# Units of the attention between the gate products in pairs, turned four slots behind their scores and met with the values six slots behind

## The reference

```python
h = rms_norm(x, norm_mix_g)
z = h @ w_in
u, v, q, k, va, gate_a, gate_b = jnp.split(z, SPLITS, axis=-1)
ya = spatial_gating_mixer(u, v, ...) @ w_proj_a
yb = window_attention(q, k, va, q_norm_g, k_norm_g, sink) @ w_proj_b
merged = jax.nn.sigmoid(gate_a) * ya + jax.nn.sigmoid(gate_b) * yb
x = x + merged @ w_out
x = x + hierarchical_moe(rms_norm(x, norm_ffn_g), ...)

# window_attention, for one head and one block of 128 queries against 3 blocks of keys
s = jnp.einsum('bqgrd,bkgd->bgrqk', qi, ki) * scale
s = jnp.where(valid, s, NEG)
p = jax.nn.softmax(jnp.concatenate([s, sink_l], axis=-1), axis=-1)[..., :-1]
o = jnp.einsum('bgrqk,bkgd->bqgrd', p, vi)
```

## Time and profile before

| | |
|---|---|
| median of three runs | 2125.69 us (2124.58 to 2127.52) |
| the profiled execution, its own time | 2126.55 us |
| its span, first to last instruction | 2124.7 us |
| PE busy | 2085.5 us, 98% of the span |
| VectorE, ScalarE, GpSimd busy | 1278.3, 1072.9 and 466.3 us (60%, 50%, 22%) |
| chain of work that ended last | PE 48%, DMA 6%, VectorE 2%, ScalarE 2% |
| mean granted clock of TensorE | 0.997 of 2.4 GHz |

### The profile page before, as it was taken

One profiled execution on the slowest core, in us unless ns is written; L12 is line 12 of the kernel. 1 busy time (PEld: TensorE's weight loads), 2 busy tenths in 40 slices (PEclk: granted clock), 3 DMA queues, 4 the chain that ended last, 5 costly groups with the idle time before them and its releaser, 6 DMA issues.

```text
span 2124.7 us, 30272 instructions
## 1 busy us (share of the span) xinstructions
PE 2085.5 (98%) x10268; PEld 1730.8 (81%) x10268; DVE 1278.3 (60%) x1645; ACT 1072.9 (50%) x1584; POOL 466.3 (22%) x653
## 2 busy tenths in 40 slices
PE   8999999999999999999999999999999999999997
PEld 7788888888788888897888888767888788888886
DVE  5654233465554233455653434458998899999995
ACT  5453332343542332344533232137877788888884
POOL 4251011210451011203510102012222222212221
PEclk9999999999999999999999999999999999999999
DMA  8312323443123322452122225489999978996863
GB/s 230 95 41 90 99 80 99 140 168 100 59 52 122 99 80 85 168 174 70 40 90 90 80 83 195 174 302 380 378 371 361 363 283 275 380 386 239 317 237 68
DMA packets 108658, 379.46 MB, mean 179 GB/s; under 512 B 13506, under 2 KB 19827, under 8 KB 82964
## 3 DMA queue, kind: packets, MB, share of 16 engines
q1 hardware_dynamic: 91812, 335.64, 44.1%
q0 software_dynamic: 16752, 42.56, 7.6%
HBM read 402.78 MB, written 34.60 MB: 206 GB/s over the span
## 4 chain that ended last, share of the span: by engine, by line
PE 48%; DMA 6%; DVE 2%; ACT 2%; issue 1%; POOL 0%; POOLq 0%; SPq 0%; ACTq 0%; DVEq 0%
DMA held_wu<-w_up_e 5%; PE main L518 3%; PE main L520 3%; PE main L519 3%; PE main L1975 3%; PE main L1973 3%; PE main L1974 3%; PE aux L1973 3%; PE aux L1974 3%; PE aux L1975 3%; PE main L1987 3%; PE main L1989 2%; PE main L1988 2%; PE main L506 2%; PE main L508 2%; PE main L507 2%
## 5 line engine op out<-in xcount | busy, mean ns | idle before, releaser
L967 DVE TENSOR_TENSOR w_lo<-raw,w_hi 128x1024 fp32r<-128x1024 f32 (+1 forms) x216 | 250.4, 1180 | 317.2 <-ACT w_hi L711 317.1
L711 ACT ACTIVATE w_hi<-raw 128x1024 fp32r<-128x1024 f32 (+1 forms) x216 | 211.5, 1005 | 142.2 <-PE main L520 72.4
L518 PE MATMUL main<-e_g_hi,w_hi 128*128 128x512 f32 x576 | 237.2, 412 | 0.0
L520 PE MATMUL main<-e_g_hi,w_lo 128*128 128x512 f32 x576 | 225.9, 392 | 0.0
L519 PE MATMUL main<-e_g_lo,w_hi 128*128 128x512 f32 x576 | 225.0, 391 | 0.0
L506 PE MATMUL main<-w_hi,e_g_hi 128*128 128x512 f32 (+1 forms) x560 | 203.6, 364 | 2.3 <-DVE e_g_lo L981 2.3
L2109 DVE TENSOR_TENSOR e_d_lo<-held_wd,e_d_hi 128x2048 fp32r<-128x2048 f32 x76 | 173.5, 2288 | 45.3 <-ACT e_d_hi L2038 45.0
L508 PE MATMUL main<-w_hi,e_g_lo 128*128 128x512 f32 (+1 forms) x560 | 200.3, 358 | 0.0
L507 PE MATMUL main<-w_lo,e_g_hi 128*128 128x512 f32 (+1 forms) x560 | 200.1, 357 | 0.0
L2109 DVE TENSOR_TENSOR e_u_lo<-held_wu,e_u_hi 128x2048 fp32r<-128x2048 f32 x76 | 173.4, 2283 | 24.0 <-ACT e_u_hi L2038 24.0
L2109 DVE TENSOR_TENSOR e_g_lo<-held_wg,e_g_hi 128x2048 fp32r<-128x2048 f32 x76 | 173.6, 2284 | 5.2 <-ACT e_g_hi L2038 5.0
(11 more groups left out here) (350 smaller groups left out, 4681.2 us busy)
## 6 DMA issues: line engine op xcount, KB each, us to landing
held_wg<-w_gate_e SPq DMA_DIRECT2D x78, 1024.0 KB
held_wu<-w_up_e SPq DMA_DIRECT2D x78, 1024.0 KB
held_wd<-w_down_e SPq DMA_DIRECT2D x76, 1024.0 KB
raw<-w_in SPq DMA_DIRECT2D x120, 512.0 KB, 3.8
raw<-w_proj_b SPq DMA_DIRECT2D x24, 512.0 KB, 3.8
raw<-w_proj_a SPq DMA_DIRECT2D x24, 512.0 KB, 3.9
raw<-w_out SPq DMA_DIRECT2D x24, 512.0 KB, 4.5
raw<-w_in SPq DMA_DIRECT2D x24, 256.0 KB, 4.5
```

The source lines that it names most:

```text
L518: pe.matmul(bank[:], hi[:, k, :], mov_hi[:, k, :], start=(k == 0), stop=False)
L520: mm = pe.matmul(bank[:], lo[:, k, :], mov_hi[:, k, :], start=False, stop=(k == KT - 1))
L711: act.activation(hi, buf, ACT.Copy).then_inc(w_hi_done, 1)
L967: dve.tensor_tensor(lo, buf, hi.bitcast(F32), ALU.subtract).then_inc(w_split, 1)
```

## The change

The 38 slots of a group are handed out as 19 pairs: three pairs in each of the first three tiles, behind the slices k = 2, 5 and 7, and two pairs in each of the others, behind k = 3 and 7. A slot is now S of unit s, T of unit s - 4, V of unit s - 6. The number of instructions of each kind is the same.

```diff
@@ -119,11 +119,15 @@
 SCALE = float(HD) ** -0.5
 
 
-def slots_of(c):
-
-    per, more = divmod(NU + 5, KT)
+
+TURNED, MET = 4, 6
+
+
+def pairs_of(c):
+
+    per, more = divmod((NU + MET) // 2, KT)
     start = per * c + min(c, more)
-    return range(start, start + per + (c < more))
+    return [(2 * i, 2 * i + 1) for i in range(start, start + per + (c < more))]
 
 
 class Arena:
@@ -337,8 +341,8 @@
 
     def gate_steps(p, j):
 
-        units = list(slots_of(4 * (p - PGB) + j))
-        steps = [("unit", s) for s in units]
+        pairs = pairs_of(4 * (p - PGB) + j)
+        steps = [("unit", s) for pair in pairs for s in pair]
         quarters = [("split", q) for q in SPLIT_AT[p][j]]
         if len(quarters) == 2:
             steps.insert(2, quarters[1])
@@ -346,7 +350,7 @@
         elif quarters:
             steps.insert(2, quarters[0])
         for k, i in (Q_STEPS.get(j, {}) if p == PGB else {}).items():
-            steps.insert(steps.index(("unit", units[k * len(units) // KT])), ("q", i))
+            steps.insert(steps.index(("unit", pairs[k * len(pairs) // KT][0])), ("q", i))
         return steps
 
     def h2_of(g, t):
@@ -508,9 +512,8 @@
                 mm = pe.matmul(bank[:, 0:n], stat_lo(k), hi[:, k, 0:n], start=False, stop=(k == KT - 1))
             return mm
 
-        def feature_major(g, bank, mov_hi, mov_lo, p, j, ready=None, slots=()):
-
-            slots = list(slots)
+        def feature_major(g, bank, mov_hi, mov_lo, p, j, ready=None, pairs=()):
+
             hi, lo = w_hi[p % 2][:, :, j * P:(j + 1) * P], w_lo[p % 2][:, :, j * P:(j + 1) * P]
             for k in range(KT):
                 if ready is not None:
@@ -518,8 +521,9 @@
                 pe.matmul(bank[:], hi[:, k, :], mov_hi[:, k, :], start=(k == 0), stop=False)
                 pe.matmul(bank[:], hi[:, k, :], mov_lo[:, k, :], start=False, stop=False)
                 mm = pe.matmul(bank[:], lo[:, k, :], mov_hi[:, k, :], start=False, stop=(k == KT - 1))
-                for s in slots[k * len(slots) // KT:(k + 1) * len(slots) // KT]:
-                    attend(g, s)
+                for pair in pairs[k * len(pairs) // KT:(k + 1) * len(pairs) // KT]:
+                    for s in pair:
+                        attend(g, s)
             return mm
 
         def kT_tile(g, t):
@@ -551,15 +555,15 @@
                 bank = take(s % 2, (s_masked, NU * g + s + 1))
                 pe.matmul(bank[:, 0:len(ch) * P].rearrange("p (c q) -> p c q", c=len(ch)), qT[:, h, n * P:(n + 1) * P],
                           kT[:, n + ch[0]:n + ch[-1] + 1, h // REP, :], start=True, stop=True).then_inc(s_ps, 1)
-            if 0 <= s - 3 < NU:
-                u = s - 3
+            if 0 <= s - TURNED < NU:
+                u = s - TURNED
                 pe.wait_ge(p_ready, NU * g + u + 1)
                 bank = take_bank(pt_bank[u % 2], (pt_ready, NU * g + u + 1))
                 for c in range(len(chunks(g, u % GT))):
                     mm = pe.transpose(bank[:, c * P:(c + 1) * P], pr[u % 4][:, c * P:(c + 1) * P], ident)
                 mm.then_inc(pt_ps, 1)
-            if 0 <= s - 5 < NU:
-                u = s - 5
+            if 0 <= s - MET < NU:
+                u = s - MET
                 h, n = divmod(u, GT)
                 ch = chunks(g, n)
                 pe.wait_ge(pt_ready, NU * g + u + 1)
@@ -677,7 +681,7 @@
                     else:
                         mm = feature_major(g, bank, hT_hi, hT_lo, p, j,
                                            (lambda k: (ready(k), turn_q(k))) if first else turn_q,
-                                           slots=slots_of(4 * (p - PGB) + j) if p in (PGB, PGB + 1) else ())
+                                           pairs=pairs_of(4 * (p - PGB) + j) if p in (PGB, PGB + 1) else ())
                     mm.then_inc(out_ready, 1)
                 if g == 1 and p in (PK, PVA) and j == 3:
                     if p == PK:
```

## The result

The change is slower by a fifth of a per cent: 2132.76 us (median of 8 runs, 2128.95 to 2136.97) against 2127.57 us (8 runs, 2124.58 to 2134.98) of the kernel before. The ratio is 1.0022 with an interval of 1.0012 to 1.0031. The first three of those runs of the kernel before had a median of 2125.69, the eight lie 1.9 higher. So the number to hold against my sum of +4.5 us is the difference of the medians, 5.2 us.

The account below looks back on a forecast made before the run. PE, busy 98% of the span, was taken to bound the kernel. Per group, waits of 4.4, 4.1 and 4.1 us against 2.55, 2.2 and 2.3, less 0.34 of breaks, gave +4.5 us: 2130.2 us, range 2126.5 to 2134.5.

Parts of the forecast that it names:

- at full clock: Likeliest case, chance 0.52: the waits come as worked out and the clock does not fall, +4.5 us in all.
- the rival's clock: Rival, chance 0.25: PE's clock halves behind gathered waits in one to three groups, adding 1.6 to 4.8 us.
- the forecast's own range: Whole kernel: the range of the likeliest case alone, 2128.2 to 2132.2 us.
- Breaks: PE's changes from small pieces back to gate products: 14 fewer at 0.024 us win 0.34 us in a group.
- The dear breaks of the rival: Rival, chance 0.06: each break costs far more than 0.024 us, deciding from 0.13; at 0.25 the kernel takes 2120.7.
- Tile 0, scores of unit 4: PE waits 2.15 us for the mask of unit 2; 2.2 us of earlier waits gathered in one, nothing won.
- Tile 1, turn 5: New wait: turn 5 writes `main0` and needs the tanh of tile 0; PE waits 1.9 us, bounds 1.5 to 2.2.
- Tile 2, turn 7: PE waits for the tanh of tile 1: 0.25 us, between 0 and 0.5.
- Further on: Behind tile 2, the spacing of pairs hides everything.
- The tanh hidden after all: Rival, chance 0.17: tanh causes no wait or PE's loss is given back later; -1.2 to +2 us, about 2126.

Follow-up runs that it names:

- experiment 1: Changed kernel with turns 5, 6 and 7 of the queries one slice later, behind the pair they stood ahead of: 2128.85 us against 2128.12 before, ratio 1.0001.
- experiment 2: Changed kernel with ScalarE taking the tanh of tiles 0 and 1 of the first panel ahead of the tile's last E: 2128.51 us, ratio 1.0000 to before.
- experiment 5: Changed kernel with only the split of quarter 1 in tile 0 moved behind unit 3 instead of unit 1: 2136.47 us against 2128.42 before, ratio 1.0044.
- experiment 6: Kernel before, single slots at distances 3 and 5, with turns 5 to 7 and the split of quarter 1 later: 2126.91 us, ratio 0.9997.
- experiment 4: Changed kernel with turns 5 to 7 one slice later and the split of quarter 1 behind unit 3: 2120.51 us against 2128.12 before, ratio 0.9964.
- experiment 3: Changed kernel with 38 single slots instead of pairs, at distances 4 and 6: 2130.03 us, ratio 1.0014 to the kernel before.
- experiment 7: Single slots at distances 4 and 6, with turns 5 to 7 and the split of quarter 1 later: 2128.09 us, ratio 1.0002 to the kernel before.

## Why the prediction held

**The sign and the size.** Forecast +4.5 us with a range of 2126.5 to 2134.5; the difference of the medians is 5.2, the median 2132.76. The mechanism of the forecast (waits gathered in one chain, and a new one for the tanh) is shown, by experiments 1, 2 and 5. But the likeliest case was written "at full clock", and the profile has the rival's clock beside it; 2132.76 lies 0.6 above the forecast's own range, with the kernel before itself 1.9 higher. That the size came out so near is in part luck: the fallen clock added 0.65 us where it might have added 1.6 for each of its two falls, and the terms of the breaks and of turn 5 were both too large and pull opposite ways.

**Breaks, −0.34 a group.** The sign may be right, the size was not: this is the term of the sum that was mis-sized. Experiments 6 and 4 differ by 20 breaks a group: 37 slots and turns 5, 6 and 7 alone make 40 in the one, 19 pairs and turn 4 alone make 20 in the other. With the noted waits taken off, the stages differ by 0.48, 0.66 and 0.63 us, which looks like 0.024 to 0.033 a break. But a noted wait begins at the modelled end of the product ahead, 0.17 us late, and waits too short to be noted are missing. So go through PE's starts one by one and take off whatever lies more than 0.04 us above the usual distance of that kind of instruction. What is left of the three stages is then 89.93, 94.21 and 94.24 us in experiment 6, 89.91, 94.03 and 94.05 in experiment 4: 0.00 to 0.01 a break. The kernel before (37 breaks) leaves 89.89, 94.31 and 94.30, so at most 0.017. The 14 breaks were worth between nothing and 0.2 us a group. The 0.02 us that the prediction read off six gate products belongs to the products: inside the stages they start 0.230 us apart and in the plain tile 0.227, with many breaks as with few (0.230 in experiment 6, 0.229 to 0.231 in experiment 4). The dear breaks of the rival (0.13 and more) are out.

**Tile 0, scores of unit 4: 2.15 us.** From 97.64 to 99.79 by forecast; measured from 97.78 (the last product starts at 97.55 and is worth 0.23) to 99.87, so 2.09. The profile notes 1.93, since it counts from the product's modelled end. Held. The copy of turn 4 came at 93.25, ahead of the E of both units, and the whole chain as much earlier as the step said.

**Tile 1, turn 5: 1.9 us.** In group 1 the profile notes 1.50 us, which counted from starts is 559.61 − 557.71 − 0.23 = 1.67 (the product ahead starts at 557.71); the stage came out at 98.18 for 98.2. Held in group 1, with the size 0.2 high. In group 0 it was only 0.50, and in group 2 it is not noted at all. There the step was wrong about PE's arrival: at half clock the work between the two waits took 1.5 us longer (in group 0 from 99.87 to 104.65, 4.78 us, where group 1 has 3.25), and PE used up the wait of turn 5 in it. The stage stayed at its forecast (group 2) or rose by 0.65 (group 0), because the slow scores of unit 5 delayed mask, E and tanh as well (0.54 us: 104.59 for 104.05).

**Tile 2, turn 7: 0.25 us.** The profile notes 0.29 and 0.19 us, and nothing in group 2; counted from starts it is 0.46, 0.35 and 0.23. Held, within its bounds of 0 to 0.5.

**Further on.** In no kernel at distances 4 and 6 has PE a noted wait behind tile 2. Held.

**The clock.** This was the rival with 0.25, at +1.6 us a fall. It fell in two groups of three of the profiled execution. The forecast kept to full clock since neither wait was as long as the 3.31 us of the earlier trace rows; that argument failed: the waits behind which it fell were of 1.93 and 1.96 us. Its price was also mis-stated, as one that always comes on top: a fall cost 1.5 to 1.75 us where PE had no wait behind it worth speaking of (experiments 1 and 5), 1.2 in group 2 of experiment 2, where turn 5 had some 0.3 us to give, and 0 to 0.65 in the change, where it lay ahead of a long wait. The 0.65 of group 0 is nearly all that separates 4.5 from 5.2.

**The tanh hidden after all, 0.17.** Out: where it is taken off PE's path (experiments 1 and 2), the stages fall from 291.3 us in sum to 287.7 and 287.2. So it was not hidden in the change.

What stays open: why the clock falls behind some waits of about 2 us and not behind others (below). No experiment varied that alone.

## What to carry to other kernels

When waits stand one behind another in a chain of three engines, look at the last of them first. Removing the first alone only passed it on: the one behind it grew from 1.50 to 3.55 us in group 1, and the kernel was the slowest of all (experiment 5). Removing the last alone won 3.6 us in the stages (experiment 1), and removing both made the kernel 7.6 us faster than the one before (experiment 4). A wait that has gathered others can also cost more than its length, since the clock fell behind all three waits of over 3.4 us.

Where an order of units is changed, look for what else is placed relative to it by fixed numbers (`Q_STEPS`, the place of a split): it was not the pairs that were slow but what stayed where the single slots had wanted it.

And compare stages, not spans. The span of the change was 2.4 us longer where its stages were 5.2 longer. Over the nine versions here the difference in the stages lies within 0.1 to 1.1 us of the difference of the medians, that of the spans within 0.1 to 2.8.

## What the runs showed of the hardware

**Behind waits of about 2 us the clock fell in some places and not in others.** All noted waits of PE over 1.6 us in the attention stages, with what the granted clock did behind each:

| wait, us | where | clock behind it |
|---|---|---|
| 1.67 to 1.89 | six, in the change and experiments 1, 2, 3 and 7 | full, six times |
| 1.93, 1.93, 1.96, 1.98, 1.98 | groups 0 and 2 of the change and of experiment 1, group 2 of experiment 2 | half (0.50) |
| 1.93, 1.93, 1.94, 2.00 | experiments 2, 7, 7 and 3 | full |
| 3.45, 3.55, 3.61 | experiment 5 | half, three times |

The Trainium skill, page "TensorE: Matmul & The Clock Gate", section "Why this matters for your kernels", warns of long idle gaps between bursts of matmuls. The three waits of 3.45 to 3.61 us agree. For waits of about 2 us the runs go both ways: five times half, four times full, so the length alone doesn't tell. Nor does the fall come at a fixed distance behind the wait: in group 0 of the change the granted clock was 0.53 over the first 1.4 us (99.87 to 101.27), in group 2 it was still 1.00 over the first microsecond (1000.03 to 1001.03) and then 0.50.

**A fall can be free.** In group 2 of the change 3.20 us at half clock (the row 1001.13:1004.33 above) left the stage 0.01 us from the forecast for full clock, since turn 5 would have stood there anyway.

**A fall needs no wait.** In the kernel before, the granted clock was 0.50 from 1210.10 to 1213.09, behind four-column products that started 0.11 us apart without a pause; in the change it stayed at 1.00 at the same place (1209.76 to 1218.34).
